# Stick-breaking running sums by pairs of heads, from split logarithms, in one-pass products

## The chip, the cores and the metric

The kernel runs on one core of one Trainium2 chip. The metric is the device time in microseconds (us) of one execution of the whole program: lower is better. TensorE (PE in the profile) multiplies, VectorE (DVE) and ScalarE (ACT) work element by element, and SyncE (SP) issues the DMAs that bring the weights.

## The reference, cut to what matters

The program is two blocks, each of two layers, over 256 tokens with 1024 channels. In a layer of the second block the normed input is projected, three attentions run on the projections (stick-breaking with 6 heads, a causal softmax with 6 heads, a softmax over 256 memory tokens with 4 heads), each output is gated, and one product brings them back to 1024 channels. The change is in the stick-breaking attention:

```python
z = einsum('bhqd,bhkd->bhqk', qb, kb) * scale
past = arange(q1)[None, :] < arange(q0, q1)[:, None]
log_beta = log_sigmoid(z)
log_one_minus = where(past, log_beta - z, 0.0)
later = cumsum(log_one_minus, axis=3, reverse=True) - log_one_minus
w = where(past, exp(log_beta + later), 0.0)
out = einsum('bhqk,bhkd->bhqd', w, vb)
```

The cumulative sum over the keys is a product with a triangular matrix of ones on TensorE.

## The kernel before, in words

Every engine has its own instruction list, written out by hand, and engines meet at counting semaphores. A function such as `stick_sums(pe, h)` issues its instructions on one engine; the order of the calls in the four lists of `stage_mix2` (L2439 on for TensorE, L2509 on for ScalarE, L2628 on for VectorE) is the order of the work.

**Weights.** They arrive in chunks of 128x2048 numbers. A chunk has two pieces of 1024 columns. ScalarE rounds a piece to a reduced 32-bit type (`split_hi`, L271, tile `w_hi`); VectorE subtracts that from the original (`split_lo`, L277, `w_lo`). A weight product is then three one-pass products, high by high, high by low and low by high (`proj_part`, L2145 to L2152; `out_part`, L2177 to L2179). Two chunks of raw weights and two of split ones fit, so the DMA of a chunk starts when the chunk two before it is split, and a chunk is split when TensorE has used the one two before it. In `stage_mix2` the chunks 0 to 15 are projections (10 and 11 are those of the memory tokens), and 16 to 19 are the output.

**Stick-breaking.** The key is on the partitions. A head has 384 columns: the first 128 keys by 256 queries, then the last 128 keys by 128 queries. `stick_scores` makes the scores; ScalarE takes the absolute value (`stick_abs`), VectorE scales and masks (`stick_masked`, tile `sb_z`). By halves of three heads (1152 columns) ScalarE then runs `stick_exp` (L2241) and `stick_log` (L2246), each after a table load, and VectorE `stick_softplus`: two operations (L2256, L2257), of which the second multiplies by a mask of -1 and 0 into the tile `sb_lom`. `stick_sums(pe, h)` runs for one head, on full 32-bit operands: 256 columns by the triangle (`trisb`, L2211), 128 by all ones (L2212), 128 by the triangle (L2213). The trace keeps two records for each such product. `stick_args` (L2261) adds `sb_z` on VectorE, `stick_weights` (L2250) is the exponential, `stick_values` the product with the values. Sums of even heads are in PSUM bank 4, of odd heads in bank 5.

**Order around it.** TensorE: chunk 9, scores of the softmax, chunk 10 with more scores, sums 0 and 1, chunk 11, sums 2 and 3, the transposes of the first softmax group (`soft_turn`, L572, which waits at its start for both divisions of `soft_div`, L560), a quarter of chunk 12, sums 4 and 5, and then the values. VectorE: piece 0 of chunk 9, `stick_softplus(1)`, piece 1 of chunk 9, pieces of chunk 10, row maxima (`soft_max`, L539, L541), pieces of chunk 11, arguments 0 and 1, divisions, pieces of chunk 12. In layer 0 alone VectorE and ScalarE also norm the memory tokens here (`mem_squares`, `mem_root` L2398, `mem_diagonal` L2414, `mem_row`) and scale the residual (`x_scale`, L495).

Of the kernel before, what the change touches and what calls it, by code (L numbers as in the profile page):

```python
# [38 lines left out]
KT = D // P  # L39
# [23 lines left out]
N_PT2 = 22  # L63
# [578 lines left out]
def stage_mix1(K, block, c, layer, norm, after, first):  # L642
# [454 lines left out]
    def lat_scores_pe(pe, t):  # L1097
        if t == 0:
            pe.wait_ge(*at("lat_roped", 2))
        else:  # L1100
            pe.wait_ge(*at("yb_lo", 1))
# [394 lines left out]
    def ya_lo(dve):  # L1496
        dve.wait_ge(*at("ya_hi", 1))
        V.tensor_tensor(MLO[:, 0:2, :], YC[:, :, :], MHI[:, 0:2, :].bitcast(fp32), ALU.subtract).then_inc(*up("ya_lo"))

    def yb_lo(dve):  # L1500
        dve.wait_ge(*at("yb_hi", 1))
        V.tensor_tensor(MLO[:, 2:4, :], two(banks[4][:, :]), MHI[:, 2:4, :].bitcast(fp32),
                        ALU.subtract).then_inc(*up("yb_lo"))

    def yc_lo(dve):
        for i in range(2):
            dve.wait_ge(*at("yc_hi", i + 1))
            V.tensor_tensor(MLO[:, 4 + 2 * i:6 + 2 * i, :], two(banks[4 + i][:, :]),
                            MHI[:, 4 + 2 * i:6 + 2 * i, :].bitcast(fp32), ALU.subtract).then_inc(*up("yc_lo"))
# [35 lines left out]
    def _(pe):  # L1545
# [88 lines left out]
        pe.wait_ge(*at("ya_lo", 1))  # L1634
# [5 lines left out]
        pe.wait_ge(*at("yc_lo", 2))  # L1640
# [442 lines left out]
def stage_mix2(K, block, c, layer, norm, after, second, out):  # L2083
# [13 lines left out]
    PJ = K.sb("proj2", [P, N_PT2, T], c=c)  # L2097
# [3 lines left out]
    R1, R2 = K.sb("rope_c", [P, 2, T], c=c), K.sb("rope_d", [P, 2, T], c=c)  # L2101
# [113 lines left out]
    def stick_values(pe, i):  # L2215
# [3 lines left out]
        pe.wait_ge(*at("sb_w", 2 * i + 2))  # L2219
# [125 lines left out]
    def gate(act, p):  # L2345
# [3 lines left out]
        S.activation(GT[:, 2 * p:2 * p + 2, :], PJ[:, S_GATE + 2 * p:S_GATE + 2 * p + 2, :], ACT.Silu,  # L2349
# [73 lines left out]
    def evacuate(dve, q):  # L2423
# [16 lines left out]
    def _(pe):  # L2440
# [69 lines left out]
    def _(act):  # L2510
# [27 lines left out]
        mem_hi(act, range(4, 8))  # L2538
# [449 lines left out]
```

## Time and profile before

| what | value |
|---|---|
| time, median of 3 runs | 940.28 us (938.91 to 940.81) |
| span of the profiled execution | 938.7 us |
| TensorE busy | 916.4 us, 98% of the span |
| VectorE busy | 680.7 us, 73% |
| ScalarE busy | 555.8 us, 59% |
| mean granted TensorE clock | 0.997 |

The span runs from the first instruction to the last; the run times also hold the start and end around it. The median of the runs is 1.6 us above the span of the profiled execution, for which no other time is given. Instructions overlap by a little, so in the rows below the distance from one start to the next is often shorter than the duration shown.

### The profile page before, as it was taken

The numbers are of one execution on the slowest core, as the hardware profiler recorded it, in microseconds if no ns is written. First come the engines' busy times: TensorE is split into PE (matmuls) and PEld (weight loads), VectorE is DVE, ScalarE is ACT, GpSimd is POOL, SyncE is SP. The second block draws the span as 40 slices with busy tenths as digits, with TensorE's granted clock in tenths as the row PEclk, the third lists the DMA queues.
The fourth block names the chain that finished last, engine by engine and source line by source line (L and its number), as shares of the span: only waits on it lengthen the run. The fifth ranks groups of instructions, "written<-read, shape, count | busy, mean of one in ns | idle before, by whom it ended". The sixth has DMA issues, their size and how long they took to land.

```text
span 938.7 us, 20423 instructions
## 1 busy us (share of the span) xinstructions
PE 916.4 (98%) x8848; PEld 869.5 (93%) x8848; DVE 680.7 (73%) x972; ACT 555.8 (59%) x851; POOL 7.6 (1%) x12
## 2 busy tenths in 40 slices
PE   8899999999999999999999999999999999999996
PEld 7788799999999999878999999999989899989896
DVE  6899667866664589976777666448799679588675
ACT  6873566654443588355754544338587667585665
POOL 0010000000000001000000000000000000000000
PEclk9999999999999999999999999999999999999998
DMA  8342115665554544211466655554544335444231
GB/s 324 151 174 95 48 56 188 214 261 183 201 201 180 180 163 151 98 64 46 140 251 232 250 192 182 204 197 135 179 136 138 132 135 180 147 168 157 93 135 67
DMA packets 24169, 150.94 MB, mean 161 GB/s; under 512 B 2960, under 2 KB 3472, under 8 KB 7056
## 3 DMA queue, kind: packets, MB, share of 16 engines
q1 hardware_dynamic: 24080, 149.64, 44.7%
q8 instruction: 70, 1.15, 0.5%
q14 instruction: 19, 0.16, 0.0%
HBM read 147.26 MB, written 1.05 MB: 158 GB/s over the span
## 4 chain that ended last, share of the span: by engine, by line
PE 67%; DVE 20%; ACT 7%; issue 3%; SPq 1%; DMA 1%; DVEq 0%; ACTq 0%
PE bank L1914 9%; PE bank L1912 8%; PE bank L1913 8%; DVE w_lo L277 6%; PE bank L2145 4%; PE bank L1936 3%; PE bank L1934 3%; PE bank L1935 3%; PE bank L2146 3%; PE bank L2147 3%; ACT w_hi L271 2%; PE bank L1075 1%; PE bank L2177 1%; PE bank L589 1%; PE bank L1165 1%
## 5 line engine op out<-in xcount | busy, mean ns | idle before, releaser
L277 DVE TENSOR_TENSOR w_lo<-w_raw,w_hi 128x1024 fp32r<-128x1024 f32 x256 | 306.0, 1224 | 106.2 <-ACT w_hi L271 105.5
L271 ACT ACTIVATE w_hi<-w_raw 128x1024 fp32r<-128x1024 f32 x256 | 259.4, 1054 | 206.3 <-PE bank L1914 104.9
L1912 PE MATMUL bank<-act_hi,w_hi 128*128 128x256 f32 x704 | 194.5, 276 | 0.0
L1913 PE MATMUL bank<-act_lo,w_hi 128*128 128x256 f32 x704 | 194.3, 276 | 0.0
L1914 PE MATMUL bank<-act_hi,w_lo 128*128 128x256 f32 x704 | 194.3, 276 | 0.0
L1912 PEld LDWEIGHTS bank<-act_hi,w_hi 128*128 128x128 f32 x704 | 132.2, 188 | 0.1
L1913 PEld LDWEIGHTS bank<-act_lo,w_hi 128*128 128x128 f32 x704 | 132.2, 188 | 0.0
L1914 PEld LDWEIGHTS bank<-act_hi,w_lo 128*128 128x128 f32 x704 | 132.2, 188 | 0.0
L2145 PE MATMUL bank<-act_hi,w_hi 128*128 128x256 f32 x352 | 100.2, 285 | 0.3
L2147 PE MATMUL bank<-act_hi,w_lo 128*128 128x256 f32 x352 | 97.7, 278 | 0.0
L2146 PE MATMUL bank<-act_lo,w_hi 128*128 128x256 f32 x352 | 97.7, 278 | 0.0
L1934 PE MATMUL bank<-gated_hi,w_hi 128*128 128x256 f32 x352 | 97.2, 276 | 0.0
L1935 PE MATMUL bank<-gated_lo,w_hi 128*128 128x256 f32 x352 | 97.2, 276 | 0.0
L1936 PE MATMUL bank<-gated_hi,w_lo 128*128 128x256 f32 x352 | 97.2, 276 | 0.0
L1138 PE MATMUL bank<-act_hi,w_hi 128*128 128x256 f32 x256 | 74.9, 292 | 3.1 <-DVE w_lo L227 1.8
L1139 PE MATMUL bank<-act_lo,w_hi 128*128 128x256 f32 x256 | 71.2, 278 | 0.0
L1140 PE MATMUL bank<-act_hi,w_lo 128*128 128x256 f32 x256 | 71.2, 278 | 0.0
L2145 PEld LDWEIGHTS bank<-act_hi,w_hi 128*128 128x128 f32 x352 | 66.5, 189 | 3.9 <-DVE w_lo L277 2.1
L2146 PEld LDWEIGHTS bank<-act_lo,w_hi 128*128 128x128 f32 x352 | 66.1, 188 | 0.0
L2147 PEld LDWEIGHTS bank<-act_hi,w_lo 128*128 128x128 f32 x352 | 66.1, 188 | 0.0
L1935 PEld LDWEIGHTS bank<-gated_lo,w_hi 128*128 128x128 f32 x352 | 66.1, 188 | 0.0
L1936 PEld LDWEIGHTS bank<-gated_hi,w_lo 128*128 128x128 f32 x352 | 66.1, 188 | 0.0
(367 smaller groups left out, 1982.1 us busy)
## 6 DMA issues: line engine op xcount, KB each, us to landing
w_raw<-in_w_ffn SPq DMA_DIRECT2D x66, 1024.0 KB, 4.8
w_raw<-in_w_mix SPq DMA_DIRECT2D x62, 1024.0 KB, 4.9
small_w<-in_small SPq DMA_DIRECT2D x2, 1280.0 KB, 7.6
w_raw<-in_w_mix SPq DMA_DIRECT2D x8, 256.0 KB, 6.3
x_res<-in_x_channels SPq DMA_DIRECT2D x4, 256.0 KB, 6.1
probs<-in_w_mix SPq DMA_DIRECT2D x2, 512.0 KB, 7.5
probsT<-in_w_mix SPq DMA_DIRECT2D x1, 1024.0 KB, 10.1
mem<-in_mem_channels SPq DMA_DIRECT2D x1, 1024.0 KB, 7.2
```

What stands on the lines that cost most here:

```text
L271: self.nc.scalar.activation(hi, self.piece(self.raw_slot(g), p), ACT.Copy).then_inc(self.hi_ready, 1)
L277: self.nc.vector.tensor_tensor(lo, self.piece(self.raw_slot(g), p), hi.bitcast(fp32), ALU.subtract).then_inc(self.lo_ready, 1)
L1138: TE.matmul(o, hi[:, w], HI[:, k, :], start=(k == 0 and x == 0), stop=False)
L1912: TE.matmul(o, hi[:, w], HI[:, k, :], start=(k == 0 and x == 0), stop=False)
L1913: TE.matmul(o, hi[:, w], LO[:, k, :], start=False, stop=False)
L1914: last = TE.matmul(o, lo[:, w], HI[:, k, :], start=False, stop=(k == KT - 1 and x == 1))
L1934: TE.matmul(out, hi[:, w], GHI[:, k, :], start=(k == 0 and o % 2 == 0), stop=False)
L1935: TE.matmul(out, hi[:, w], GLO[:, k, :], start=False, stop=False)
L1936: last = TE.matmul(out, lo[:, w], GHI[:, k, :], start=False, stop=(k == FK - 1 and o % 2 == 1))
L2145: TE.matmul(o, hi[:, w], h[:, k, :], start=(k == 0 and x == 0), stop=False)
L2146: TE.matmul(o, hi[:, w], l[:, k, :], start=False, stop=False)
L2147: last = TE.matmul(o, lo[:, w], h[:, k, :], start=False, stop=(k == KT - 1 and x == 1))
```

## The change

The running sums are made for two heads at a time (three calls instead of six). The masked logarithm, now kept in `sb_l`, is split like a weight piece: `stick_hi` on ScalarE rounds three heads (1152 columns) into `sb_lom_hi`, `stick_lo` on VectorE writes the rest into `sb_lom_lo`. The triangle and the ones are brought to the reduced type once (`sum_consts`, two 128x128 copies on ScalarE in layer 0). A pair is then six one-pass products: 512 columns by the triangle for high and low, 256 by the ones for each, 256 by the triangle for each. `stick_args` is two additions for each pair (512 and 256 columns), `stick_weights` one exponential of 768 columns. The sums, additions and exponential of a pair stand where those of its two heads stood. Buffers are laid out anew (the gates' projections in a tile of their own over the memory of `sb_lom_lo`; the final norm's rows go to `sb_l`), and in the first mixing block three pairs of semaphores become one pair (`y_hi`, `y_lo`) with the counts adapted; the order of its work is the same.

```diff
-    def stick_sums(pe, h):
-        pe.wait_ge(*at("sb_lom", 1 + h // 3))
-        if h < 2:
+    def stick_sums(pe, i):
+        pe.wait_ge(*at("sb_lo", 1 + (2 * i + 1) // 3))
+        if i == 0:
             pe.wait_ge(*at("sb_abs", 6))
             pe.wait_ge(*at("sb_zm", 6))
+            pe.wait_ge(sem("sum_consts"), 2)
         else:
-            pe.wait_ge(*at("sb_arg", h - 1))
-        o = banks[4 + h % 2]
-        TE.matmul(o[:, 0:T], cst("trisb"), LM[:, h, 0:T], start=True, stop=False)
-        TE.matmul(o[:, P:T], cst("ones"), LM[:, h, T:384], start=False, stop=True)
-        TE.matmul(o[:, T:384], cst("trisb"), LM[:, h, T:384], start=True, stop=True).then_inc(*up("sb_sum"))
+            pe.wait_ge(*at("sb_arg", 2 * i))
+        w, heads = slice(2 * i, 2 * i + 2), two(banks[4][:, :])
+        last_keys = banks[5][:, 0:T].rearrange("p (j t) -> p j t", j=2)
+        for n in range(2):
+            TE.matmul(heads, SUMS[:, 0, :], LMS[n][:, w, 0:T], start=(n == 0), stop=False)
+        for n in range(2):
+            TE.matmul(heads[:, :, P:T], SUMS[:, 1, :], LMS[n][:, w, T:384], start=False, stop=(n == 1))
+        for n in range(2):
+            last = TE.matmul(last_keys, SUMS[:, 0, :], LMS[n][:, w, T:384], start=(n == 0), stop=(n == 1))
+        last.then_inc(*up("sb_sum"))
...
-    def stick_weights(act, h):
-        act.wait_ge(*at("sb_arg", h + 1))
-        S.activation(LL[:, h, :], LL[:, h, :], ACT.Exp, bias=cst("zero")).then_inc(*up("sb_w"))
+    def stick_weights(act, i):
+        act.wait_ge(*at("sb_arg", 2 * i + 2))
+        w = slice(2 * i, 2 * i + 2)
+        S.activation(LL[:, w, :], LL[:, w, :], ACT.Exp, bias=cst("zero")).then_inc(*up("sb_w"))
+
+    def sum_consts(act):
+        act.wait_ge(sem("second_in"), 16)
+        act.wait_ge(sem("scaled_rms_sum"), 1)
+        S.activation(SUMS[:, 0, :], cst("trisb"), ACT.Copy).then_inc(sem("sum_consts"), 1)
+        S.activation(SUMS[:, 1, :], cst("ones"), ACT.Copy).then_inc(sem("sum_consts"), 1)
...
-        ch(V.tensor_tensor(LM[:, w, :], LL[:, w, :], BC("sbneg", 3), ALU.mult), "sb_lom")
-
-    def stick_args(dve, ch, h):
-        dve.wait_ge(*at("sb_sum", h + 1))
-        ch.post(V.tensor_tensor(LL[:, h, :], banks[4 + h % 2][:, 0:384], ZS[:, h, :], ALU.add), "sb_arg")
+        ch(V.tensor_tensor(LL[:, w, :], LL[:, w, :], BC("sbneg", 3), ALU.mult), "sb_lom")
+
+    def stick_hi(act, x):
+        act.wait_ge(*at("sb_lom", x + 1))
+        w = slice(3 * x, 3 * x + 3)
+        S.activation(LMS[0][:, w, :], LL[:, w, :], ACT.Copy).then_inc(*up("sb_hi"))
+
+    def stick_lo(dve, x):
+        dve.wait_ge(*at("sb_hi", x + 1))
+        w = slice(3 * x, 3 * x + 3)
+        V.tensor_tensor(LMS[1][:, w, :], LL[:, w, :], LMS[0][:, w, :].bitcast(fp32),
+                        ALU.subtract).then_inc(*up("sb_lo"))
+
+    def stick_args(dve, ch, i):
+        dve.wait_ge(*at("sb_lo", 2))
+        dve.wait_ge(*at("sb_sum", i + 1))
+        w = slice(2 * i, 2 * i + 2)
+        ch.post(V.tensor_tensor(LL[:, w, 0:T], two(banks[4][:, :]), ZS[:, w, 0:T], ALU.add), "sb_arg")
+        ch.post(V.tensor_tensor(LL[:, w, T:384], banks[5][:, 0:T].rearrange("p (j t) -> p j t", j=2), ZS[:, w, T:384],
+                                ALU.add), "sb_arg")
...
         stick_sums(pe, 0)
+        proj(pe, 11)
         stick_sums(pe, 1)
-        proj(pe, 11)
-        stick_sums(pe, 2)
-        stick_sums(pe, 3)
         soft_turn(pe, 0)
         proj(pe, 12, (0,))
-        stick_sums(pe, 4)
-        stick_sums(pe, 5)
+        stick_sums(pe, 2)
...
         mem_hi(act, range(4, 8))
+        if layer == 0:
+            sum_consts(act)
         stick_exp(act, 0)
...
         st.split_hi(act, 9, 0)
+        stick_hi(act, 0)
         stick_log(act, 1)
         st.split_hi(act, 9, 1)
...
         st.split_hi(act, 10, 0)
+        stick_hi(act, 1)
         st.split_hi(act, 10, 1)
...
         st.split_lo(dve, 9, 0)
+        stick_lo(dve, 0)
         stick_softplus(dve, ch, 1)
         st.split_lo(dve, 9, 1)
         if layer == 0:
             mem_diagonal(dve, ch)
         st.split_lo(dve, 10, 0)
+        stick_lo(dve, 1)
         st.split_lo(dve, 10, 1)
...
         stick_args(dve, ch, 0)
-        stick_args(dve, ch, 1)
         soft_div(dve, ch, 0, 0)
         st.split_lo(dve, 12, 0)
         soft_div(dve, ch, 0, 1)
         st.split_lo(dve, 12, 1)
+        stick_args(dve, ch, 1)
+        st.split_lo(dve, 13, 0)
         stick_args(dve, ch, 2)
-        stick_args(dve, ch, 3)
-        st.split_lo(dve, 13, 0)
-        stick_args(dve, ch, 4)
-        stick_args(dve, ch, 5)
```

## Rows read from the trace of the kernel before

**Rows 1.** The page: busy time of each engine, and engines of the last chain.

```profile
PE 916.4 (98%) x8848; PEld 869.5 (93%) x8848; DVE 680.7 (73%) x972; ACT 555.8 (59%) x851; POOL 7.6 (1%) x12
...
PE 67%; DVE 20%; ACT 7%; issue 3%; SPq 1%; DMA 1%; DVEq 0%; ACTq 0%
```

**Rows 2.** Windows in layers 0 and 1: length, then busy us of PE, PEld, DVE, ACT, POOL.

```profile
700.00:740.00 40.00, 39.84 (x331) 36.20 (x330) 32.18 (x60) 27.98 (x60) 0.00 (x0) 1.00 0.36 119
...
844.00:884.00 40.00, 39.84 (x334) 36.57 (x333) 27.92 (x49) 24.12 (x55) 0.00 (x0) 1.00 0.37 132
```

**Rows 3.** Timeline of TensorE, layer 0: start, us, engine, line, operation, count, idle before.

```profile
688.02 1.98 PE L2333 MATMUL bank<-proj,consts_both 128*128 128x512 f32 x4
...
715.92 0.28 PE L2147 MATMUL bank<-mem_hi,w_lo 128*128 128x256 f32 x1
716.04 0.59 PE L2211 MATMUL bank<-sb_lom,consts_second 128*128 128x256 f32 x2
...
716.92 0.60 PE L2211 MATMUL bank<-sb_lom,consts_second 128*128 128x256 f32 x2
...
717.72 0.36 PE L2150 MATMUL bank<-w_hi,mem_hi 128*128 128x256 f32 x1
```

**Rows 4.** Groups by line over the span: busy us, mean ns, then idle before.

```profile
L2211 PE MATMUL bank<-sb_lom,consts_second 128*128 128x256 f32 x24 | 7.1, 379 | 0.0
L2250 ACT ACTIVATE sb_l<-sb_l,prm 128x384 f32<-128x384 f32 x12 | 6.7, 615 | 1.6 <-DVE sb_l L2261 1.6
L2261 DVE TENSOR_TENSOR sb_l<-bank,sb_z 128x384 f32<-128x384 f32 x12 | 6.3, 552 | 2.3 <-PE bank L2213 2.3
...
L2257 DVE TENSOR_TENSOR sb_lom<-sb_l,consts_second 128x1152 f32<-128x1152 f32 x4 | 5.4, 1358 | 0.1
```

**Rows 5.** Timeline of VectorE, layer 0, up to chunk 10.

```profile
685.49 1.36 DVE L2256 SCALAR_TENSOR_TENSOR sb_l<-sb_z,sb_l 128x1152 f32<-128x1152 f32 x1 [0.63 <-issue]
...
703.81 1.23 DVE L277 TENSOR_TENSOR w_lo<-w_raw,w_hi 128x1024 fp32r<-128x1024 f32 x1
706.00 0.17 DVE L2414 RECIPROCAL mem_rs<-mem_rs 128x2 f32<-128x2 f32 x1 [0.96 <-ACT mem_rs L2398]
...
706.95 2.36 DVE L277 TENSOR_TENSOR w_lo<-w_raw,w_hi 128x1024 fp32r<-128x1024 f32 x2 [0.27 <-ACT w_hi L271]
```

**Rows 6.** TensorE's weight loads after a wait, chunk 9 piece 1, both layers.

```profile
705.09 0.19 PEld L2145 LDWEIGHTS bank<-act_hi,w_hi 128*128 128x128 f32 x1 [0.33 <-DVE w_lo L277]
...
847.88 0.19 PEld L2145 LDWEIGHTS bank<-act_hi,w_hi 128*128 128x128 f32 x1 [0.34 <-DVE w_lo L277]
```

**Rows 7.** Timeline of ScalarE, layer 0.

```profile
696.59 1.06 ACT L271 ACTIVATE w_hi<-w_raw 128x1024 fp32r<-128x1024 f32 x1 [2.21 <-PE bank L2152]
697.67 1.28 ACT L2246 ACT_TABLE_LOAD   x1
698.96 1.26 ACT L2246 ACTIVATE sb_l<-sb_l,prm 128x1152 f32<-128x1152 f32 x1
...
714.96 0.41 ACT L549 ACTIVATE probs<-probs,neg_max 128x128 f32<-128x128 f32 x1 [1.73 <-DVE neg_max L541]
```

**Rows 8.** Timeline of VectorE, layer 0: chunks 11 and 12, last division.

```profile
714.84 2.35 DVE L277 TENSOR_TENSOR w_lo<-w_raw,w_hi 128x1024 fp32r<-128x1024 f32 x2
...
722.74 1.23 DVE L277 TENSOR_TENSOR w_lo<-w_raw,w_hi 128x1024 fp32r<-128x1024 f32 x1 [0.58 <-ACT w_hi L271]
...
724.09 1.14 DVE L560 TENSOR_SCALAR probs<-probs,exp_sum 128x256 f32<-128x256 f32 x4
```

**Rows 9.** Timeline of TensorE, layer 0: transposes of the first softmax group.

```profile
725.38 0.85 PE L572 MATMUL bank<-consts_both,probs 128*128 128x128 f32 x6
```

**Rows 10.** Timeline, layer 1: last division on VectorE, then TensorE's transposes.

```profile
863.17 1.14 DVE L560 TENSOR_SCALAR probs<-probs,exp_sum 128x256 f32<-128x256 f32 x4
...
867.57 1.47 PE L572 MATMUL bank<-consts_both,probs 128*128 128x128 f32 x12
```

**Rows 11.** Timeline of VectorE, layer 0: its first work on the third softmax group.

```profile
741.08 1.29 DVE L536 TENSOR_SCALAR probs<-bank 128x512 f32<-128x512 f32 x2 [3.16 <-PE bank L572]
```

More of the change, by code:

```diff
@@ L1100, in lat_scores_pe @@
         else:
-            pe.wait_ge(*at("yb_lo", 1))
+            pe.wait_ge(*at("y_lo", 1))
         n, tok = LAT_KT[t], slice(t * P, (t + 1) * P)
@@ L1309, in ya_hi @@
         act.wait_ge(*at("ya_out", 1))
-        S.activation(MHI[:, 0:2, :], YC[:, :, :], ACT.Copy).then_inc(*up("ya_hi"))
+        S.activation(MHI[:, 0:2, :], YC[:, :, :], ACT.Copy).then_inc(*up("y_hi"))
     def yb_hi(act):
         act.wait_ge(*at("values", 1))
-        S.activation(MHI[:, 2:4, :], two(banks[4][:, :]), ACT.Copy).then_inc(*up("yb_hi"))
+        S.activation(MHI[:, 2:4, :], two(banks[4][:, :]), ACT.Copy).then_inc(*up("y_hi"))
     def yc_hi(act):
@@ L1318, in yc_hi @@
         for i in range(2):
-            S.activation(MHI[:, 4 + 2 * i:6 + 2 * i, :], two(banks[4 + i][:, :]), ACT.Copy).then_inc(*up("yc_hi"))
+            S.activation(MHI[:, 4 + 2 * i:6 + 2 * i, :], two(banks[4 + i][:, :]), ACT.Copy).then_inc(*up("y_hi"))
     def evacuate(dve, q):
@@ L1496, in ya_lo @@
     def ya_lo(dve):
-        dve.wait_ge(*at("ya_hi", 1))
-        V.tensor_tensor(MLO[:, 0:2, :], YC[:, :, :], MHI[:, 0:2, :].bitcast(fp32), ALU.subtract).then_inc(*up("ya_lo"))
+        dve.wait_ge(*at("y_hi", 2))
+        V.tensor_tensor(MLO[:, 0:2, :], YC[:, :, :], MHI[:, 0:2, :].bitcast(fp32), ALU.subtract).then_inc(*up("y_lo"))
     def yb_lo(dve):
-        dve.wait_ge(*at("yb_hi", 1))
+        dve.wait_ge(*at("y_hi", 1))
         V.tensor_tensor(MLO[:, 2:4, :], two(banks[4][:, :]), MHI[:, 2:4, :].bitcast(fp32),
-                        ALU.subtract).then_inc(*up("yb_lo"))
+                        ALU.subtract).then_inc(*up("y_lo"))
     def yc_lo(dve):
         for i in range(2):
-            dve.wait_ge(*at("yc_hi", i + 1))
+            dve.wait_ge(*at("y_hi", i + 3))
             V.tensor_tensor(MLO[:, 4 + 2 * i:6 + 2 * i, :], two(banks[4 + i][:, :]),
-                            MHI[:, 4 + 2 * i:6 + 2 * i, :].bitcast(fp32), ALU.subtract).then_inc(*up("yc_lo"))
+                            MHI[:, 4 + 2 * i:6 + 2 * i, :].bitcast(fp32), ALU.subtract).then_inc(*up("y_lo"))
     @block.sync
@@ L1633, in _ @@
         lat_turn_probs_pe(pe)
-        pe.wait_ge(*at("ya_lo", 1))
+        pe.wait_ge(*at("y_lo", 2))
         out_part(pe, 1, 0)
@@ L1639, in _ @@
         out_part(pe, 1, 3)
-        pe.wait_ge(*at("yc_lo", 2))
+        pe.wait_ge(*at("y_lo", 4))
         for q in (2, 3):
@@ L2096, in stage_mix2 @@
     MV = K.sb("mem_v", [P, NT, 256], c=c)
-    PJ = K.sb("proj2", [P, N_PT2, T], c=c)
+    with ExitStack() as shared:
+        LML = K.sb("sb_lom_lo", [P, 6, 384], f32r, shared)
+    GP = K.sb("gate_proj", [P, 8, T], c=c)
+    R1, R2 = K.sb("rope_c", [P, 2, T], c=c), K.sb("rope_d", [P, 2, T], c=c)
+    PJ = K.sb("proj2", [P, S_GATE, T], c=c)
     PV = K.sb("proj2_v", [P, 3, NT, 256], c=c)
@@ L2100, in stage_mix2 @@
     OUT = PJ[:, 0:8, :]
-    R1, R2 = K.sb("rope_c", [P, 2, T], c=c), K.sb("rope_d", [P, 2, T], c=c)
+    SUMS = second["sums"]
     SQUARES = att.PR[:, 0, :, :].rearrange("p x n -> p (x n)")
@@ L2107, in stage_mix2 @@
     LL = K.sb("sb_l", [P, 6, 384], c=c)
-    LM = K.sb("sb_lom", [P, 6, 384], c=c)
+    LMS = (K.sb("sb_lom_hi", [P, 6, 384], f32r, c), LML)
     if layer == 1:
-        after.buffers(*(x.rearrange("p h n -> p (h n)")[:, 0:KT * T] for x in (ZS, LM)))
+        after.buffers(*(x.rearrange("p h n -> p (h n)")[:, 0:KT * T] for x in (ZS, LL)))
     value2 = lambda col, w, s: PV[:, col // 256, s, col % 256:col % 256 + w]
@@ L2218, in stick_values @@
             projected(pe, Q_V + 1)
-        pe.wait_ge(*at("sb_w", 2 * i + 2))
+        pe.wait_ge(*at("sb_w", i + 1))
         for h in (2 * i, 2 * i + 1):
@@ L2427, in evacuate @@
         else:
-            tile = 2 * q if q < Q_V else S_MEQ if q == Q_MEQ else S_GATE + 2 * (q - Q_GATE)
-            dst, row = PJ[:, tile:tile + 2, :], K.RSB
+            tile = 2 * q if q < Q_V else S_MEQ if q == Q_MEQ else 2 * (q - Q_GATE)
+            dst, row = (PJ if q < Q_GATE else GP)[:, tile:tile + 2, :], K.RSB
         V.tensor_tensor(dst, two(proj_bank(q)[:, :]), spread(row), ALU.mult).then_inc(*up("projected"))
@@ L2565, in _ @@
         stick_weights(act, 0)
-        stick_weights(act, 1)
         st.split_hi(act, 12, 1)
@@ L2569, in _ @@
         soft_copy(act, 0)
-        stick_weights(act, 2)
-        stick_weights(act, 3)
+        stick_weights(act, 1)
         st.split_hi(act, 13, 0)
         st.split_hi(act, 13, 1)
-        stick_weights(act, 4)
-        stick_weights(act, 5)
+        stick_weights(act, 2)
         soft_out(act, 0)
@@ L2862, in program @@
             second["mem_rs"] = K.sb("mem_rs", [P, NT], c=c, top=True)
+            with ExitStack() as shared:
+                second["sums"] = K.sb("sum_consts", [P, 2, P], f32r, shared, top=True)
             SQ2 = K.sb("scaled_squares", [P, 3, 512], c=c, top=True)
```

3 lines of the change are left out of this document (1 added, 2 removed).

## The prediction

> **What bounds the kernel now.** First the page: which engine is busy, and which one the chain of waits runs through. TensorE is busy for 98% of the span, yet only 67% of the last chain is its own and 20% is VectorE's [rows 1]. So TensorE has hardly a gap, but many of its instructions start just when VectorE lets them: the two are nearly tied, and a load taken from one and put on the other can come out with either sign. Then the windows around the running sums: in 40 us TensorE is busy for 39.84 in both layers, VectorE for 32.18 in layer 0 and 27.92 in layer 1 [rows 2]. VectorE has 4.3 us more to do in layer 0 (the memory tokens' norm and the residual's scale). The layers have to be judged apart, and by the places where TensorE really waits for VectorE, which the timelines show.
>
> **TensorE: what the sums cost.** Sums of two heads begin at 716.04 and 716.92, 0.88 us apart [rows 3], so a pair costs 1.76 us and the twelve heads of both layers 10.6 us. One head streams 256 + 128 + 128 = 512 columns, 1.72 ns for each. A one-pass weight product of 256 columns starts 0.12 us before what follows it (715.92 to 716.04) [rows 3], 0.47 ns a column. A pair streams, high and low, 2 x (512 + 256 + 256) = 2048 columns after the change: 0.96 us at that rate. No one-pass product of 512 columns is in the trace. Its cost lies between that of 256 columns, 0.12 us, and that of a full-precision product of 512, at most 0.99 us (1.98 for two) [rows 3]; since the full-precision ones cost in proportion to their columns (0.88 for 512 in three products), I take 0.24. A pair gets 0.8 us cheaper, a layer 2.4, both 4.8.
>
> The Trainium skill (VectorE: DVE Perf Modes, the errata section's cycle table) gives a matmul as 6 cycles plus its columns at 2.4 GHz, an estimate of 0.216 us for 512. By it a pair would cost 0.91 us and the two layers' saving would be 5.1 us in place of 4.8. No row here shows such a product.
>
> **VectorE: what is added.** `stick_lo` is two subtractions of 1152 columns in a layer. The product of the same size (L2257) has a mean of 1.36 us [rows 4], a piece of 1024 takes 1.18 (2.36 for two) [rows 5]; between those I take 1.3 each, 2.6 a layer. The additions change little: six of 0.55 us [rows 4], 3.3 us, against three of 512 and three of 256 columns over the same total columns. I take nothing. Six exponentials of 0.62 us [rows 4] become three wide ones, on ScalarE; they lie under chunk 12's products, and with no cover each would delay `stick_values` by less than its own length.
>
> **ScalarE: what is added.** `stick_hi` rounds 1152 columns twice a layer. Rounding 1024 takes 1.08 us from start to start, an exponential over 1152 takes 1.26 [rows 7]; I take 1.15, between them. `sum_consts` is two copies of 128x128 in layer 0; one of that size takes 0.41 [rows 7], a lower bound on their place is nothing; I take 0.6 for both. They stand ahead of `stick_exp(0)`, and the first softplus begins only when the logarithm is there (0.63 us idle) [rows 5], so VectorE is later by all of 0.6 from there on.
>
> **First meeting, chunk 9 piece 1.** TensorE waits for this piece in both layers: its load at 705.09 and at 847.88 follows VectorE's `w_lo` directly [rows 6]; in layer 0 VectorE began it at 703.81 for 1.23 us [rows 5]. `stick_lo(0)` stands ahead of it. `stick_hi(0)` and the longer wait for the logarithm behind it are over by then. So TensorE is later here by 1.3 us in layer 1 and by 1.3 + 0.6 = 1.9 in layer 0. Queued behind the waiting product are all of chunks 9 and 10 and the sums.
>
> **Second meeting, layer 0: the transposes.** `soft_turn` waits for both divisions. The last begins in a group at 724.09 that lasts 1.14 us, and the transposes begin at 725.38 [rows 8, 9]: no slack, 0.15 us is the signal's way. How late is VectorE there? Its inverse root at 706.00 waited 0.96 us for ScalarE, the next weight piece another 0.27 [rows 5]. ScalarE is later by `stick_hi(0)`, 1.15; that takes over, for VectorE's own 1.9 are cut by 1.2 us of waiting. Behind it `stick_lo(1)` adds 1.3. Together 2.45. From there on VectorE is full up to 722.74, where it waits 0.58 for ScalarE [rows 8], whose exponentials hang on VectorE's own maxima and move with them. So the division, and with it the transposes, come 2.45 us later: TensorE, which gained 0.8 on each of the first two pairs, stands idle for 2.45 - 1.9 + 1.6 = 2.15 us before them. Chunk 11's pieces, split from 714.84 for 2.35 us and used from 717.72 [rows 3, 8], are no meeting of their own: the first is later by 2.45 and ready at about 718.5, and TensorE comes at 717.72 + 1.9 - 0.8 = 718.8. After the transposes the third pair gives back 0.8. Layer 0: +2.45 - 0.8 = +1.65 us.
>
> **Second meeting, layer 1.** No memory norm stands there. The last division ends at 864.31 and the transposes begin at 867.57 [rows 10]: 3.26 us of slack. Even 2.6 us of `stick_lo` fit. TensorE is later by 1.3 from chunk 9 and gains 0.8 three times. Layer 1: +1.3 - 2.4 = -1.1 us.
>
> **Afterwards.** At 741.08 VectorE has been idle for 3.16 us, waiting for TensorE's next transposes [rows 11]: there its lateness ends, and all that follows in the layer hangs on TensorE again. So each layer's sum is carried to the end unchanged. The buffers' new places and the shared semaphores in the first block add no instruction and change no order: nothing, and as the waits are for the same events I see no loss either. No DMA is added; chunk 11's comes later with chunk 9's split and is covered by that of VectorE.
>
> **The sum.** +1.65 - 1.1 = +0.55 us on a span of 938.7; the median of the runs stands 1.6 above that span, so 940.28 + 0.55 = 940.8. Likeliest: about the same time, with 4.8 us less work on TensorE and 5.3 us more on VectorE. A measurement of this kernel tells a change from none at about 0.2%, 1.9 us.
>
> **The rivals.**
> - *The meeting in layer 0 has more room than I count* (ScalarE's copy is quicker, VectorE closes the 0.58 us and its other small waits). Then layer 0 is like layer 1: 2 x -1.1 = -2.2, 938.1 us. For it: VectorE has 7.8 idle us in that window [rows 2]. Against it: the transposes start 0.15 us after the last division [rows 8, 9]. 19%.
> - *The saving comes through whole*, as the busy shares alone would have it: VectorE at 73% hides what is added. -4.8, 935.5 us. Against it: two loads that follow `w_lo` directly [rows 6]. 9%.
> - *Slower: VectorE's lateness reaches the transposes in layer 1 too.* One mechanism: the added split in front of chunk 10 and its copy on ScalarE hold VectorE by more than the slack. It decides once the last division there is later by 3.26 us less the 0.3 that TensorE comes earlier (1.3 - 1.6), so by about 3. Then layer 1 loses what layer 0 loses, and 2 x +1.65 gives 943.6 us. For it: 2.6 + 1.15 = 3.75 us of added work on the two engines in series at most. Against it: VectorE waits for DMA-fed pieces there and has 12 idle us in the window [rows 2]. 17%.
> - *The change doesn't do what it says: the wide products run at the old rate.* Then a pair is 2048 columns at 1.72 ns, 3.5 us in place of 1.76: six pairs +10.6, about 951 us at the least. The weight products, of the same type, argue against it. 5%.
>
> **How the numbers follow.** My forecast has 50%; the rivals take the other 50. The range should leave out 2 in 10 at most: the whole saving (9%) and the old rate (5%) are outside, as well as a few per cent beyond the ends of the bounds. From 938.1 less an uncertainty of 1.1 (`stick_lo` between 1.18 and 1.36, `stick_hi` between 1.08 and 1.26, the wide product) to 943.6: 937.0 to 943.6. The forecast's own range is 939.2 to 942.2. Faster by over 0.2% (below 938.4): the whole saving, more than half of the first rival and a few of my own cases, 24%. Slower (above 942.2): the third and fourth rivals and 4 from my own, 26%. The same: 50%.
>
> **What the profile after would show.** The pair's six products in 0.9 to 1.0 us, L2257's successor and the new subtraction at 1.3 to 1.4 us, the copies at 1.1 to 1.2. TensorE's wait for chunk 9 piece 1 grows from 0.33 us to about 1.1 in layer 0 and 0.5 in layer 1, with another of 1.15 ahead of piece 0, since `values_sb(7)` stands behind `stick_hi(0)` on ScalarE and frees the bank. Ahead of the transposes TensorE idles about 2 us in layer 0 and not at all in layer 1. What would make me wrong: a transposes' wait in layer 1, none in layer 0, or a wide product far from 0.24 us.

## The result, and the profile after

The changed kernel takes 942.96 us (median of 5 runs, 942.87 to 944.11) against 940.26 us (5 runs, 938.91 to 940.81) for the kernel before, 2.7 us more. The ratio, from runs taken side by side, is 1.0033 with a 95% interval of [1.0021, 1.0045], which is 3.1 us. A second comparison of the same two kernels (below) gave 1.0022 [1.0014, 1.0031]. The time lies inside the predicted range, but beyond the forecast's own 942.2 us and beyond the 0.2% that a measurement tells from no change (the second comparison lies just at that bound): what came is "slower" (26%), not "about the same" (50%). Three single executions among all the series were far longer than the rest (1137, 3183 and 5150 us); the medians and ratios below are without them.

The page of the changed kernel, busy times and chain:

```profile
span 941.2 us, 20358 instructions
...
PE 914.1 (97%) x8812; PEld 866.1 (92%) x8812; DVE 685.6 (73%) x976; ACT 559.2 (59%) x851; POOL 7.6 (1%) x12
...
PE 64%; DVE 20%; ACT 9%; issue 3%; DMA 2%; SPq 1%; DVEq 0%; ACTq 0%
```

Against [rows 1] VectorE has 4.9 us more to do, ScalarE 3.4 and TensorE 2.3 less, and TensorE's part of the chain fell from 67% to 64%. The records of pipelined products overlap, so the saving on TensorE is read from start to start, in the timeline of TensorE at the first pair (start, duration, instruction):

```profile
718.45 0.40 PE L2218 MATMUL bank<-sb_lom_hi,sum_consts 128*128 128x512 f32 x1
718.69 0.39 PE L2218 MATMUL bank<-sb_lom_lo,sum_consts 128*128 128x512 f32 x1
718.91 0.28 PE L2220 MATMUL bank<-sb_lom_hi,sum_consts 128*128 128x256 f32 x1
...
719.39 0.28 PE L2153 MATMUL bank<-w_hi,mem_hi 128*128 128x256 f32 x1
```

A pair takes 719.39 - 718.45 = 0.94 us (it was 1.76 [rows 3]), a one-pass product of 512 columns 0.22 to 0.24. TensorE did get its 0.82 us for each pair, 4.9 in all.

TensorE's weight loads that waited (in brackets how long, and for what) around layer 0's and layer 1's chunk 9, the transposes (L571) and the scores after them (L2323):

```profile
703.78 0.19 PEld L2148 LDWEIGHTS bank<-act_hi,w_hi 128*128 128x128 f32 x1 [1.55 <-ACT proj_v L2418]
707.26 0.19 PEld L2148 LDWEIGHTS bank<-act_hi,w_hi 128*128 128x128 f32 x1 [0.67 <-DVE w_lo L276]
...
728.44 1.29 PEld L571 LDWEIGHTS bank<-consts_both,probs 128*128 128x128 f32 x12 [2.50 <-issue]
...
736.13 0.30 PEld L2323 LDWEIGHTS bank<-proj 64*128 64x128 f32 x4 [0.51 <-ACT proj L2402]
...
849.08 0.19 PEld L2148 LDWEIGHTS bank<-act_hi,w_hi 128*128 128x128 f32 x1 [1.26 <-ACT proj_v L2418]
852.45 0.19 PEld L2148 LDWEIGHTS bank<-act_hi,w_hi 128*128 128x128 f32 x1 [0.57 <-DVE w_lo L276]
...
878.20 0.30 PEld L2323 LDWEIGHTS bank<-proj 64*128 64x128 f32 x4 [0.51 <-ACT proj L2402]
```

Chunk 9's first piece now waits in both layers for a bank that `values_sb(7)` frees late, its second piece for `w_lo`, and layer 0's transposes stand 2.50 us behind the last division; all of that was forecast. The wait of 0.51 for `proj` was not.

**How each layer's own cost is read.** The same instruction is found in both traces, and its start in the one of before is taken from its start in the one of after. What this shift gains between the ends of a stretch is that stretch's own cost; its value before the stretch is scatter or an earlier change. For VectorE's subtractions of weight pieces that begin before the change at 678.27 and 773.96 us (layer 0) and at 835.85 and 916.20 us (layer 1), the shift of the changed kernel is +0.50, +2.59, +3.30 and +2.42. So layer 0 costs +2.1 us, layer 1 gives -0.9, and 0.5 + 0.7 us are from elsewhere: in this profile 0.64 came in the first block, and 0.77 between the layers where the first weight piece after a DMA started late. The kernel before itself, run again, showed neither jump, and lay at -0.84 to -0.86 at all four of these places. The same reading for every profile, beside the ratio of all its runs:

| kernel | layer 0 | layer 1 | idle before layer 0's transposes | granted clock, 727 to 731 | mean clock of all runs | ratio |
|---|---|---|---|---|---|---|
| before, again | 0.0 | 0.0 | 0.14 | 1.00 | .9958 | 1.0005 [0.9996, 1.0014] |
| after | +2.1 | -0.9 | 2.50 | 1.00 | .9948 | 1.0033 [1.0021, 1.0045] |
| after, again | +3.4 | -0.9 | 2.52 | 0.67 | .9952 | 1.0022 [1.0014, 1.0031] |
| pairs, full precision | 0.0 | -0.15 | 0.45 | 1.00 | .9961 | 0.9999 [0.9990, 1.0007] |
| high part only | +2.5 | -2.4 | 2.99 | 0.62 | .9953 | 1.0000 [0.9991, 1.0008] |
| residual's scale later | -0.4 | -0.7 | none | 1.00 | .9956 | 0.9988 [0.9979, 0.9996] |
| the same move in before | -0.1 | 0.0 | none | 1.00 | .9962 | 0.9998 [0.9989, 1.0007] |
| splits later | +3.5 | -1.7 | 2.51 | 0.81 | .9948 | 1.0020 [1.0012, 1.0029] |
| output copy first | +3.4 | -1.25 | 2.49 | 0.57 | .9949 | 1.0024 [1.0016, 1.0033] |
| idle products | +2.2 | -0.9 | 0.82 | 1.00 | .9959 | 1.0011 [1.0002, 1.0020] |
| scale later, copy first | -0.8 | -1.3 | none | 1.00 | .9960 | 0.9979 [0.9970, 0.9988] |
| all moves | -1.2 | -2.4 | 1.38 | 1.00 | .9962 | 0.9954 [0.9941, 0.9966] |
| split on GpSimd | +4.4 | -2.6 | 0.98 | 1.00 | .9938 | 1.0022 [1.0013, 1.0032] |

The idle column is TensorE's wait, in us, ahead of its load for the transposes; layer columns are in us; the mean clock is that of 5 to 12 runs; the kernel before, over 35 runs in each of the first two series, has .9964. The GpSimd kernel in the last row had its low clock earlier, from 721.6 us.

### The profile page after: what moved, and what is told of

The parts are those of the page before. It is cut to its first block, busy times and chain, and to the rows that moved or that the text cites. A ratio compares the mean times of both kernels' runs of the same rounds, so it can differ in the third digit from the quotient of the medians.

```text
span 941.2 us, 20358 instructions
## 1 busy us (share of the span) xinstructions
PE 914.1 (97%) x8812; PEld 866.1 (92%) x8812; DVE 685.6 (73%) x976; ACT 559.2 (59%) x851; POOL 7.6 (1%) x12
## 4 chain that ended last, share of the span: by engine, by line
PE 64%; DVE 20%; ACT 9%; issue 3%; DMA 2%; SPq 1%; DVEq 0%; ACTq 0%
PE bank L1911 9%; PE bank L1913 8%; PE bank L1912 8%; DVE w_lo L276 6%; PE bank L1933 3%; PE bank L1935 3%; PE bank L1934 3%; PE bank L2148 3%; PE bank L2149 3%; PE bank L2150 3%; ACT w_hi L270 3%; DMA w_raw<-in_w_mix 1%; PE bank L1074 1%; PE bank L1164 1%; PE bank L1165 1%
```

## The experiments

Each edit is one of the changed kernel, unless it says otherwise.

### Both kernels again

No edit.

> The kernel before, unchanged, measured as if it were a change. Ratio 1.000 within 0.0015. In the profile after the change two jumps stand outside the running sums: +0.64 us between 379 and 424 us (first block) and +0.77 us where layer 1 begins (about 782 us), both behind a weight DMA. If they are scatter of single executions, some profiles of unchanged kernels show them and others don't; if they belong to the change, this profile shows neither.

> The changed kernel once more. Ratio to the kernel before 1.002 to 1.0045. My account of its first profile: +2.1 us in layer 0, -0.7 in layer 1, +1.2 outside the running sums. If the 1.2 is scatter of the DMA landings, this profile has other jumps there, and the two layers' own parts stay within 0.3 us. If it is the change's own (other buffer addresses, merged semaphores), the same two jumps come again.

Measured: 940.78 us (1.0005) and 941.98 us, 1.0022 [1.0014, 1.0031]. The loss is real, and some 2 to 3 us. The second profile of the changed kernel has the same waits, and layer 1 keeps its part, but layer 0 costs 3.4 us instead of 2.1, 1.3 more where at most 0.3 was expected. Transposes in the timelines of TensorE, first the changed kernel, then the same kernel again:

```profile
728.47 1.50 PE L571 MATMUL bank<-consts_both,probs 128*128 128x128 f32 x12 [2.32 <-DVE probs L559]
```

```profile
727.87 2.32 PE L571 MATMUL bank<-consts_both,probs 128*128 128x128 f32 x12 [2.34 <-DVE probs L559]
```

The same twelve products take 2.32 us instead of 1.50. The windows of the second profile say why (length, busy times of PE, PEld, DVE, ACT, POOL with their counts, granted clock, DMA share and GB/s):

```profile
727.00:728.00 1.00, 0.13 (x1) 0.16 (x2) 1.00 (x4) 0.69 (x2) 0.00 (x0) 1.00 0.00 0
728.00:729.00 1.00, 1.00 (x8) 1.00 (x8) 1.00 (x2) 0.54 (x2) 0.00 (x0) 0.70 0.00 0
729.00:730.00 1.00, 1.00 (x7) 1.00 (x6) 0.79 (x2) 0.85 (x2) 0.00 (x0) 0.50 0.38 66
730.00:731.00 1.00, 1.00 (x6) 1.00 (x6) 0.00 (x0) 0.85 (x3) 0.00 (x0) 0.50 0.70 172
731.00:735.00 4.00, 4.00 (x35) 3.43 (x33) 2.16 (x3) 2.72 (x4) 0.00 (x0) 0.90 0.50 207
```

After the idle time the granted clock fell to 0.5, the lower level of 1.2 GHz, for about 3.4 us (the windows from 728 on lose 0.3, 0.5, 0.5 and 4 x 0.1 us of full clock, 1.7 in all, at half the clock). The layer's cost with it is 3.4 - 2.1 = 1.3 us higher.

### Merging alone: pairs in full 32-bit products

No split and no constants in the reduced type; a pair is three full-precision products.

```diff
-        for n in range(2):
-            TE.matmul(heads, SUMS[:, 0, :], LMS[n][:, w, 0:T], start=(n == 0), stop=False)
+        TE.matmul(heads, cst("trisb"), LM[:, w, 0:T], start=True, stop=False)
...
-        stick_hi(act, 0)
...
-        stick_lo(dve, 0)
```

> The pairing alone: products on full 32-bit operands for two heads at a time, merged additions and exponentials, no rounding, no subtraction, no converted constants. My theory: a pair still costs 1.76 us on TensorE, nothing is added elsewhere, and only the new wait shows (scores of the second softmax group behind the output copy, which stands behind the wide exponential), 0.4 us a layer: +0.8 us, ratio 1.001. Rival (the merging is what costs): the ratio of the change itself, 1.003. Rival (merging is free): 1.000.

Measured: 939.95 us, 0.9999 [0.9990, 1.0007]. Three calls instead of six, wide exponentials and additions, the new buffers and the shared semaphores cost nothing by themselves that this comparison resolves (0.7 us at the most by the interval), so the loss is in the split. The wait for the output copy, which I expected here, did not come; likely it needs a TensorE that arrives earlier, which no run tests by itself.

### The high part only

The low part of the logarithms is left out of the sums, with its subtraction. ScalarE's rounding stays.

```diff
-        stick_lo(dve, 0)
...
-        stick_lo(dve, 1)
```

> The low part left out: no subtraction on VectorE, three products a pair in place of six (the sums lose their low part). My theory (TensorE waits for VectorE at chunk 9 and, in layer 0, at the transposes): TensorE saves another 2.8 us and the two meetings are nearer by the subtractions, so 4.5 to 5 us less than the changed kernel, about 938.2 us, ratio to the kernel before 0.998. Rival (VectorE's added work is hidden and the loss has another cause): only the products' 2.8 us, about 940.2 us, ratio 1.000.

Measured: 940.27 us, 1.0000 [0.9991, 1.0008], where 0.998 was expected. Layer 1 does what the theory says (-2.4). Layer 0 does not: +2.5, where I had counted on +0.3. The clock fell at its transposes (0.62 in the table), which in the changed kernel went with 1.3 us; about 1.2 us is left for the waits. Timeline of VectorE in it:

```profile
706.99 0.17 DVE L2443 RECIPROCAL mem_rs<-mem_rs 128x2 f32<-128x2 f32 x1 [1.74 <-ACT mem_rs L2427]
...
709.94 1.23 DVE L276 TENSOR_TENSOR w_lo<-w_raw,w_hi 128x1024 fp32r<-128x1024 f32 x1 [0.77 <-ACT w_hi L270]
```

The inverse root waits 1.74 us for ScalarE (0.96 in [rows 5]), and the second piece of chunk 10 another 0.77, for `stick_hi(1)` stands ahead of its rounding. The last division's group begins at 725.94 for 724.09 [rows 8], with -0.35 brought along, so 2.20 us late, against 2.59 in the changed kernel. So ScalarE's two copies alone make VectorE late there, and the subtractions of 1.3 us mostly fill its waits. My working came to nearly the same lateness by another road: it took the first copy through `mem_root` and added `stick_lo(1)`, and in the changed kernel that road is there (chunk 10's first piece begins at 708.78 for 706.95, with 0.50 brought along 1.33 us late, and `stick_lo(1)` adds its 1.27). But the second copy, ahead of chunk 10's second rounding, is a road of nearly the same length, and taking `stick_lo` away leaves it.

### The residual's scale later, in the changed kernel and in the one before

`x_scale`, eight operations and 3.26 us of VectorE in layer 0, moves from ahead of chunk 11's pieces to behind the second softmax group.

```diff
-            norm.x_scale(dve, range(KT))
...
         soft_div(dve, ch, 1, 1)
+        if layer == 0:
+            norm.x_scale(dve, range(KT))
```

> The changed kernel with the residual's scaling (eight operations on VectorE, 3.26 us, layer 0) moved from ahead of the first softmax group's maxima to behind the last division of the second group, where VectorE idles. My theory: in layer 0 TensorE waits 2.3 us before the transposes because VectorE is 2.6 us late there; 3.26 us less ahead of them ends the wait, and with it the stretch at half clock that followed it in two of three profiles. 2.3 to 2.9 us less than the changed kernel, ratio to the kernel before 0.9990 to 1.0000. Rival (ScalarE's copies hold the transposes, not VectorE's load): no more than 0.5 us less, ratio 1.002.

> Control: the same move in the kernel before. My theory: there VectorE was just in time for the transposes, TensorE did not wait, so the move brings nothing: ratio 0.9995 to 1.0005. Rival (VectorE's load held TensorE in the kernel before as well, so the move is a gain of its own): 2 us or more less, ratio 0.998.

Measured: 939.26 us, 0.9988 [0.9979, 0.9996], and for the kernel before 0.9998 [0.9989, 1.0007]. VectorE's last division in a group and TensorE's transposes, in the timelines of the changed kernel with the move:

```profile
723.29 1.14 DVE L559 TENSOR_SCALAR probs<-probs,exp_sum 128x256 f32<-128x256 f32 x4
```

```profile
725.27 1.47 PE L571 MATMUL bank<-consts_both,probs 128*128 128x128 f32 x12
```

The division ends 0.84 us before the transposes, which wait for nothing. Layer 0 went from +2.1 or +3.4 to -0.4. The move is worth nothing in the kernel before and 2.5 to 3.8 us of layer 0 in the changed one: the place where layer 0 loses is this meeting, and its cause is VectorE's lateness.

### The splits later

Both roundings go behind `values_sb(8)` on ScalarE, both subtractions behind `soft_max(0, 0)` on VectorE: behind chunk 9 and 10, ahead of the first pair.

```diff
-        stick_hi(act, 0)
-        stick_hi(act, 1)
         values_sb(act, 8)
+        stick_hi(act, 0)
+        stick_hi(act, 1)
...
         soft_max(dve, ch, 0, 0)
+        stick_lo(dve, 0)
+        stick_lo(dve, 1)
```

> The changed kernel with both roundings on ScalarE moved behind the values of chunk 8 and both subtractions on VectorE behind the first maxima, so nothing of the split stands ahead of chunk 9. My theory: the meeting at chunk 9 is gone in both layers (1.3 us in layer 1; in layer 0 the time comes back at the transposes, or at chunk 11, since VectorE has as much to do ahead of them). 1.3 us less than the changed kernel, ratio to the kernel before about 1.001. Rival (the meeting at chunk 9 costs nothing that isn't caught up later): 1.0022 to 1.0033 as the changed kernel.

Measured: 941.74 us, 1.0020 [1.0012, 1.0029], where 1.001 was expected. Chunk 9's waits are back to those of the kernel before in layer 1 (0.21 and 0.34 us) and near them in layer 0 (0.49 and 0.39, where it had 0.21 and 0.33), and layer 1 gives 1.7 us instead of 0.9. In layer 0 a new wait took their place. Weight loads that waited there:

```profile
720.63 0.19 PEld L2153 LDWEIGHTS bank<-w_hi,mem_hi 128*128 128x128 f32 x1 [1.46 <-issue]
729.80 2.42 PEld L571 LDWEIGHTS bank<-consts_both,probs 128*128 128x128 f32 x12 [2.51 <-issue]
```

TensorE comes to chunk 11 before its pieces are split, and to the transposes 2.5 us early as before. In a layer whose VectorE is full, moving the load only moves the wait.

### The output copy ahead of the last exponential

```diff
-        stick_weights(act, 2)
         soft_out(act, 0)
+        stick_weights(act, 2)
```

> The changed kernel with the output copy of the first softmax group ahead of the last wide exponential on ScalarE. My theory: TensorE's wait of 0.5 us before the second group's scores is gone in both layers, 0.6 to 0.8 us less than the changed kernel, ratio 1.0015 to 1.0025. Rival (the last exponential becomes the wait of the stick-breaking values instead): no difference.

Measured: 942.40 us, 1.0024 [1.0016, 1.0033]. Both waits of 0.51 are gone and layer 1 gives 1.25 us instead of 0.9, the 0.4 that was expected. The total doesn't resolve it: the interval is 1.6 us wide, and it holds "no difference" (1.0022) as well. Layer 0 had the low clock in this profile (0.57), so it can't be compared with the one in which the clock held.

### Idle products ahead of the transposes

Fourteen one-pass products of 256 columns, which nothing reads, go ahead of layer 0's transposes.

```diff
         stick_sums(pe, 1)
+        if layer == 0:
+            for n in range(14):
+                TE.matmul(banks[6][:, 0:T], SUMS[:, 1, :], LMS[0][:, 0, 0:T], start=True, stop=True)
         soft_turn(pe, 0)
```

> The changed kernel, with 14 one-pass products of 256 columns into an unused bank ahead of layer 0's transposes, 1.6 us of work in TensorE's 2.3 to 2.5 us of waiting; they compute nothing that is used. My theory: the wait, 2.3 us and more of silence, is what was followed by half the clock in four of five profiles with it; with 0.8 us of silence the clock stays at 1.0 through the transposes and they take 1.5 us, not 2.2. Time 0 to 0.8 us less than the changed kernel, ratio 1.0015 to 1.0025. Rival (the clock falls for another reason): transposes at 0.5 again.

Measured: 941.82 us, 1.0011 [1.0002, 1.0020]. The transposes are no earlier (they wait for the division), but TensorE idles 0.82 us instead of 2.5, its clock stays at 1.00, and layer 0 costs +2.2 as in the one profile of the changed kernel in which the clock held. The mean clock over all runs rises from .9948 and .9952 to .9959; 0.0009 of 940 us are 0.8 us. Between the ratios lie 0.0011 to 0.0022, 1 to 2 us. So the low clock is likely a part of the loss of its own, near 1 us on the average of the runs. That average is argued, not shown: the interval overlaps that of the second comparison, the mean clocks of kernels that hardly idle there lie nearly as far apart (.9956 to .9962), and they hold other falls of the clock too (below). What is shown is the cost in single executions.

### Better versions

Scale later and output copy first; and both of them with the splits later and `sum_consts` behind `stick_exp(1)`:

```diff
-            sum_consts(act)
         stick_exp(act, 1)
+        if layer == 0:
+            sum_consts(act)
```

> The changed kernel with two moves: the residual's scaling behind the second group's last division (the x_late run, 0.9988) and the first group's output copy ahead of the last wide exponential (in the soft_out_first run layer 1 became 0.4 us shorter). My theory: both add up now that no half clock follows the transposes, 0.8 us less than x_late, ratio to the kernel before 0.9980. Rival: as x_late, 0.9988.

> All moves together: scaling late, output copy early, both roundings and both subtractions behind chunk 10, the two constants' copies behind the second exponential where ScalarE waits. My theory: what was TensorE's wait at chunk 9 (1.3 us and more a layer) is gone as well, and VectorE has room for the subtractions ahead of chunk 11 in both layers: about 3 us less than x_late, 4 us less than the kernel before, close to the 4.8 that TensorE saves. Ratio 0.9960. Rival (the subtractions now delay chunk 11 or the maxima): 0.998.

Measured: 938.47 us, 0.9979 [0.9970, 0.9988], and 936.44 us (5 runs), 0.9954 [0.9941, 0.9966]. The second beats both kernels, the one before by 3.9 us (940.31 in the runs beside it) and the changed one, by the medians, by 5.5 to 6.5. Its page:

```profile
span 933.5 us, 20359 instructions
...
PE 913.0 (98%) x8812; PEld 865.6 (93%) x8812; DVE 685.2 (73%) x976; ACT 559.1 (60%) x851; POOL 7.6 (1%) x12
```

and TensorE's loads that waited at chunk 9 and at the transposes of layer 0, then at chunk 9 of layer 1:

```profile
700.32 0.19 PEld L2148 LDWEIGHTS bank<-act_hi,w_hi 128*128 128x128 f32 x1 [0.48 <-ACT proj_v L2418]
...
723.10 1.29 PEld L571 LDWEIGHTS bank<-consts_both,probs 128*128 128x128 f32 x12 [1.38 <-issue]
...
841.90 0.19 PEld L2148 LDWEIGHTS bank<-act_hi,w_hi 128*128 128x128 f32 x1 [0.21 <-ACT proj_v L2418]
845.05 0.19 PEld L2148 LDWEIGHTS bank<-act_hi,w_hi 128*128 128x128 f32 x1 [0.34 <-DVE w_lo L276]
```

From the scale's move alone to the first of the two, which adds the copy's move, layer 0 goes from -0.4 to -0.8 and layer 1 from -0.7 to -1.3. In the second, layer 1 keeps the whole saving of its three pairs (-2.4), the wait before the second piece being the 0.34 us that the kernel before has as well [rows 6]. Layer 0 still pays 1.38 us at the transposes. The work added to each engine is the same as in the changed kernel (VectorE 685.2 and 685.6 us busy): only its places differ.

### The subtraction on GpSimd

`stick_lo` goes to GpSimd (7.6 us busy in the whole changed kernel), with the roundings and constants later and the copy first; `x_scale` stays in its place.

```diff
-        V.tensor_tensor(LMS[1][:, w, :], LL[:, w, :], LMS[0][:, w, :].bitcast(fp32),
+        nc.gpsimd.tensor_tensor(LMS[1][:, w, :], LL[:, w, :], LMS[0][:, w, :].bitcast(fp32),
                         ALU.subtract).then_inc(*up("sb_lo"))
```

> The subtractions on GpSimd in place of VectorE, roundings and constants' copies late, output copy early, but the residual's scaling where it was. An addition of 512 columns took GpSimd 1.31 us in the profile before, so 1152 columns should take about 2.9 us, hidden. My theory: VectorE is as early as in the kernel before, so layer 0 gains only the third pair (0.8 us; TensorE waits 1.6 us before the transposes) and layer 1 gains 2.4: 3.2 us less than the kernel before, ratio 0.9966. Rival (GpSimd and VectorE slow each other at the memory): VectorE's instructions beside it get longer and the ratio is 0.999 or more.

Measured: 942.27 us, 1.0022 [1.0013, 1.0032]; the rival came true. Timelines of GpSimd, then VectorE, then TensorE in layer 0:

```profile
709.97 2.98 POOL L2285 TENSOR_TENSOR sb_lom_lo<-sb_l,sb_lom_hi 128x1152 fp32r<-128x1152 f32 x1 [346.51 <-ACT sb_lom_hi L2279]
712.89 2.92 POOL L2285 TENSOR_TENSOR sb_lom_lo<-sb_l,sb_lom_hi 128x1152 fp32r<-128x1152 f32 x1
```

```profile
710.27 2.95 DVE L494 SCALAR_TENSOR_TENSOR x_res<-x_res,prm,first_rs 128x256 f32<-128x256 f32 x1
713.14 2.95 DVE L494 SCALAR_TENSOR_TENSOR x_res<-x_res,prm,first_rs 128x256 f32<-128x256 f32 x1
...
716.80 0.48 DVE L494 SCALAR_TENSOR_TENSOR x_res<-x_res,prm,first_rs 128x256 f32<-128x256 f32 x1
```

```profile
721.33 0.36 PE L2153 MATMUL bank<-w_hi,mem_hi 128*128 128x256 f32 x1 [4.25 <-DVE w_lo L276]
```

The two subtractions take 5.84 us there, and the eight operations of `x_scale` 8.21 us instead of 3.26. It is two of the eight that grow, from 0.48 to 2.95 us: one for each subtraction, and each ends 0.28 us behind it. The other six keep their length. VectorE had 2.6 us less to do and became 5 us later: TensorE waited 4.25 us for chunk 11, the clock fell after that wait, and layer 0 cost +4.4. In layer 1, without `x_scale`, the same kernel gives -2.6, the best of all.

## Why the prediction was right, and where it was not

**Right, by its terms.** A pair 0.94 us (0.96 said). `stick_lo` 1.35, with 1.27 from one start to the next (1.3), and `stick_hi` 1.16 (1.15):

```profile
L2284 DVE TENSOR_TENSOR sb_lom_lo<-sb_l,sb_lom_hi 128x1152 fp32r<-128x1152 f32 x4 | 5.4, 1352 | 0.0
```

The rival of the old rate is out with that. First meeting: in layer 1 piece 1's load came at 852.45 instead of 847.88, with 3.30 us of shift brought along, so 1.27 for 1.3; in layer 0 at 707.26 instead of 705.09 with 0.50 brought along, 1.67 for 1.9. The waits stood where the forecast put them, 1.55 us ahead of piece 0 (1.15) and 0.67 ahead of piece 1 (about 1.1) in layer 0, 1.26 and 0.57 (0.5) in layer 1. Second meeting: the transposes of layer 0 went from 725.38 to 728.47, less 0.50 brought along 2.59 us for 2.45, with 2.3 to 2.5 us of idle time for 2.15. In layer 1 they waited for nothing; the last division's group began at 867.61 and the transposes at 870.58:

```profile
867.61 1.14 DVE L559 TENSOR_SCALAR probs<-probs,exp_sum 128x256 f32<-128x256 f32 x4
```

```profile
870.58 1.47 PE L571 MATMUL bank<-consts_both,probs 128*128 128x128 f32 x12
```

Those are 1.8 us from its end at 868.75 to the transposes, where 3.26 had been [rows 10], so the slower rival (lateness through the slack in layer 1) did not come: the layer gained. The two faster ones did not come either: layer 0 had no more room, and the whole saving did not come through. And at its first work on the third softmax group VectorE again waits for TensorE (2.76 us at 743.68), so a layer's sum was carried on as said.

**The step that failed: "Six exponentials ... become three wide ones, on ScalarE; they lie under chunk 12's products".** The exponential of pair 2 begins only when both of its heads have their arguments, and `soft_out(0)` stands behind it. In the timeline of ScalarE of the changed kernel:

```profile
734.65 0.94 ACT L2261 ACTIVATE sb_l<-sb_l,prm 128x768 f32<-128x768 f32 x1 [1.28 <-DVE sb_l L2292]
735.50 0.58 ACT L2402 ACTIVATE proj<-bank 128x512 f32<-128x512 f32 x1
```

TensorE's next scores wait for that copy, 0.51 us in each layer. I looked at what needs the exponential, `stick_values`, and not at what is queued behind it. With the copy ahead layer 1 gained 0.4 us, and with the scale later as well layer 0 gained 0.4 and layer 1 0.65; in the full-precision pairs, where TensorE isn't earlier, the wait isn't there. I take 0.4 us a layer, +0.8 in the sum. The buffers and the shared semaphores, put at nothing, cost nothing that the full-precision run resolves.

**What had no term: the clock.** The forecast put TensorE idle for 2.15 us before layer 0's transposes and priced only the idle time. Of the five profiles with 2.49 us or more of idle time ahead of that load, four (the changed kernel's second, the high part only, the splits later, the copy first) ran what followed at a clock that fell to 0.5; in the changed kernel's first it held. With less idle time ahead of that load it held in every profile.

**Sizes that were off.** The work added to VectorE was put at 5.3 us, where its own terms give 2 x 2.6 = 5.2, and came to 4.9. `sum_consts` made VectorE 0.39 us later where 0.6 was said (each of its two copies takes 0.30). The first softplus began at 686.38 instead of 685.49, 0.50 of which was brought along:

```profile
686.38 1.36 DVE L2273 SCALAR_TENSOR_TENSOR sb_l<-sb_z,sb_l 128x1152 f32<-128x1152 f32 x1 [1.03 <-issue]
```

**The sum again.** Layer 0: +2.59 - 0.82 (third pair) + 0.4 = +2.2, +2.1 in the profile with the full clock. Layer 1: +1.27 - 2.46 + 0.4 = -0.8, -0.9 in both profiles. Together +1.3 where the sum had +0.55, and 1.3 us more in those executions in which the clock falls, 2.6. The two comparisons, 1.0033 and 1.0022, are 3.1 and 2.1 us. The second fits that span; the first lies 0.5 us above the sum with the low clock, and this part has no cause here beyond the scatter of the runs. The mechanism was right and its place was right; 0.8 us for the copy and, likely, about 1 for the clock on the average of the runs brought it over the bound. That a time 2 to 3 us slower still fell inside the range is owed to its upper end, which was set by the third rival, not by these two terms. Two things stay open: how often the clock falls, as only profiled executions show it, and the 0.77 us between the layers, which both profiles of the changed kernel have at the same DMA landing and the second gives back (4.04 to 3.33) before chunk 9 of layer 1; the kernel before and some of the experiments are without it, others have as much or more. The 0.64 of the first block is absent in the second profile, and is scatter.

## What to carry to other kernels

When a change moves work from the busiest engine to two others, find the places where the busiest one already waits for them, and put the added work behind those places; the same added work cost 2.7 us where it was put, and in other places of the same lists, with two older instructions moved, the kernel gained 3.9. For each instruction that grows or moves, ask who is queued behind it on its engine, and not only who reads its result. And a wait of over 2 us that opens on TensorE is to be priced with the slower clock that can follow it, 1.3 us here.

## What the hardware showed that I had not expected

**The clock after an idle stretch.** Ahead of layer 0's transposes the granted clock was 1.00 after every idle stretch up to 1.38 us (all moves). After 2.49 to 2.99 us it fell in four profiles of five, to 0.5 for 3.4 us, and held in one. In the kernel with the subtraction on GpSimd it fell to a mean of 0.66 for 5 us after the 4.25 us at chunk 11:

```profile
720.00:725.00 5.00, 3.67 (x18) 3.70 (x19) 4.97 (x7) 1.84 (x9) 0.00 (x0) 0.66 0.32 85
```

The transposes' group of 1.50 us takes 2.15 to 2.79 in the four, and the same kernel runs differently from one execution to the next. With the idle time filled with products that nothing reads, the clock stayed at 1.00 in the one profile of it.

Shorter stretches can be followed by it too. About 28 us from the start, far from the running sums, TensorE is idle for 2.1 to 2.2 us in all fourteen profiles. In eleven of them, that of the kernel before with the scale moved among them, the clock then fell to 0.5 for 3.4 us; in both profiles of the kernel before and in that of the scale later with the copy first it held. Windows of the changed kernel, then of the kernel before:

```profile
28.00:30.00 2.00, 0.04 (x2) 0.07 (x2) 1.84 (x6) 1.98 (x3) 0.00 (x0) 1.00 0.05 20
...
32.00:34.00 2.00, 2.00 (x6) 1.64 (x5) 1.93 (x5) 0.51 (x1) 0.00 (x0) 0.50 0.00 0
```

```profile
28.00:30.00 2.00, 0.37 (x4) 0.40 (x6) 1.83 (x7) 1.99 (x4) 0.00 (x0) 1.00 0.03 11
...
32.00:34.00 2.00, 1.28 (x7) 0.81 (x6) 1.97 (x4) 0.18 (x1) 0.00 (x0) 1.00 0.00 0
```

**VectorE beside GpSimd.** The two engines did not share evenly; one stood until the other's instruction was over. An operation of `x_scale` (two tiles read, 256 columns) takes 0.48 us alone; the two that began during a subtraction on GpSimd lasted 2.95 us, to just behind its end. In layer 1 a weight piece's subtraction on VectorE that began 0.12 us after GpSimd's took 3.74 us instead of 1.22, and GpSimd's second one, which began beside it, 3.71 where the first took 2.78. So one small instruction can cost its engine the length of a long one on the other. GpSimd's subtraction of 1152 columns has a mean of 3.09 us, VectorE's 1.35. The Trainium skill (GPSIMD Engine Reference, Key points) says that GpSimd contends for its memory interfaces with VectorE instructions that have two inputs in SBUF; this trace agrees, with 2.95 us for 0.48.

**The one-pass product of 512 columns** took 0.22 to 0.24 us from one start to the next. By the cycle table cited in the prediction (the Trainium skill, VectorE: DVE Perf Modes, the errata section) an estimate was 0.216; the trace lies 0.00 to 0.02 us above it. The 0.91 us that the prediction gives for a pair by that table takes only the two products of 512 columns from it, and 0.12 for each of the four of 256 from the rows; the measured 0.94 fits that.
